# Memory values moved into the cross-attention, memory weights scaled in place on POOL, end of the mixer reordered, weight slots exchanged

## What is computed

```python
def mixer_layer(x, ...):
    h = rmsnorm(x, g) @ w_in_l           # split into q, k, v, hq, hf, hi, hg, cb, cc, ch
    a = attn(q, k, v)                    # block attention, prompt and sample rows
    o_h, S = hgrn2_mixer(hq, hf, hi, hg, ...)   # recurrence, per-head rmsnorm, silu(hg) as gate
    o_c = cb * causal_dwconv(cc * ch)
    return x + concatenate([a, o_h, o_c]) @ w_out_l

def memory_kv(mem, g, wk, wv):           # 256 memory rows of the prompt, per layer
    m = rmsnorm(mem, g)
    return m @ wk, m @ wv                # both are outputs too

def cross_attn(x, g, wq, wo, mk, mv):
    q = rmsnorm(x, g) @ wq
    p = softmax(q @ mk.T * scale)
    return (p @ mv) @ wo
```

## Time and profile before

| What | Value |
|---|---|
| Median of 3 runs | 884.84 us (880.19 to 889.64) |
| Profiled execution, its time and its span | 887.91 us, 886.1 us |
| Mean granted clock of the PE | 0.982 |
| PE busy | 838.4 us, 95% of the span |
| DVE busy | 580.1 us, 65% |
| ACT busy | 456.9 us, 52% |
| POOL busy | 363.3 us, 41% |
| Share of the PE in the chain that ended last | 67% |
| Moved by DMA | 137.70 MB, mean 155 GB/s |

### The profile page before, as it was taken

The page is one execution under the profiler, slowest core; times in us unless marked ns, Lnnn a source line. Parts: engine busy times, 40 slices in busy tenths (PEclk is TensorE's granted clock), DMA queues, the critical chain, the costliest instruction groups (busy, mean ns, idle before and its releaser), DMA issues.

```text
span 886.1 us, 17206 instructions
## 1 busy us (share of the span) xinstructions
PE 838.4 (95%) x6422; PEld 780.2 (88%) x6422; DVE 580.1 (65%) x1263; ACT 456.9 (52%) x944; POOL 363.3 (41%) x330
## 2 busy tenths in 40 slices
PE   8999999897898999999999998989889899999996
PEld 6988877785798999999999997779669899999996
DVE  4778864755798877735356887386469887763342
ACT  4653553537656656534345355353664775654332
POOL 1412310533225665666742241053212565566542
PEclk9999999999999999999999999999989999999998
DMA  9765621677165565555648663149825565655432
GB/s 276 198 161 162 191 73 48 174 198 227 49 191 143 163 172 156 166 168 166 185 122 204 185 190 97 49 126 236 230 55 144 145 183 149 177 157 163 159 107 73
DMA packets 210111, 137.70 MB, mean 155 GB/s; under 512 B 23764, under 2 KB 202620, under 8 KB 210028
## 3 DMA queue, kind: packets, MB, share of 16 engines
q1 hardware_dynamic: 201024, 113.56, 45.2%
q0 software_dynamic: 8544, 22.85, 8.8%
q10 hardware_dynamic: 459, 0.18, 0.1%
HBM read 131.13 MB, written 5.44 MB: 154 GB/s over the span
## 4 chain that ended last, share of the span: by engine, by line
PE 67%; DVE 11%; issue 9%; DMA 4%; ACT 3%; POOL 3%; DVEq 1%; POOLq 1%; SPq 0%; ACTq 0%
PE banks L1278 19%; PE banks L1280 18%; PE banks L1279 18%; DVE ring_r L1820 3%; DMA ring<-in_w_up 2%; PE banks L1273 2%; POOL XG L861 1%; PE banks L1517 1%; PE banks L1417 1%; DMA ring<-in_w_in 1%; DVE phase L2092 1%; DVE phase_r L1735 1%; PE banks L1622 1%; PE banks L1316 1%; POOL XG L849 1%
## 5 line engine op out<-in xcount | busy, mean ns | idle before, releaser
L1280 PE MATMUL banks<-mix_r,ring_r 128*128 128x288 f32 x960 | 283.9, 296 | 0.0
L1280 PEld LDWEIGHTS banks<-mix_r,ring_r 128*128 128x128 f32 x960 | 181.9, 190 | 0.0
L1278 PE MATMUL banks<-mix_r,ring_r 128*128 128x288 f32 x480 | 148.5, 309 | 9.9 <-issue 6.6
L914 POOL TENSOR_TENSOR ring_r<-ring,keysT_r 128x512 fp32r<-128x512 f32 (+2 forms) x36 | 100.2, 2784 | 110.2 <-ACT keysT_r L1158 103.0
L914 POOL TENSOR_TENSOR ring_r<-ring,vals_r 128x512 fp32r<-128x512 f32 (+2 forms) x32 | 88.8, 2775 | 93.9 <-ACT vals_r L1158 93.7
L1280 PE MATMUL banks<-phase_r,ring_r 128*128 128x288 f32 x416 | 122.6, 295 | 0.0
L1158 ACT CAST ring_r<-ring 128x1024 fp32r<-128x1024 f32 x60 | 62.4, 1047 | 90.6 <-DMA ring<-in_w_in 63.2
L1278 PEld LDWEIGHTS banks<-mix_r,ring_r 128*128 128x128 f32 x480 | 91.4, 190 | 16.6 <-issue 11.8
L1279 PE MATMUL banks<-XG_r,ring_r 128*128 128x288 f32 x352 | 104.5, 297 | 0.0
L2092 DVE SCALAR_TENSOR_TENSOR phase<-banks,fpar,phase 128x255 f32<-128x255 f32 (+1 forms) x160 | 76.7, 480 | 38.1 <-ACT phase L1214 31.7
L1820 DVE TENSOR_TENSOR ring_r<-ring,keysT_r 128x1536 fp32r<-128x1536 f32 (+1 forms) x36 | 59.6, 1656 | 54.1 <-ACT keysT_r L1158 54.1
(11 more groups left out here) (315 smaller groups left out, 2061.7 us busy)
## 6 DMA issues: line engine op xcount, KB each, us to landing
ring<-in_w_up SPq DMA_DIRECT2D x88, 512.0 KB, 5.3
ring<-in_w_in SPq DMA_DIRECT2D x36, 512.0 KB, 4.3
ring<-in_w_down SPq DMA_DIRECT2D x16, 1024.0 KB, 5.3
ring<-in_w_down SPq DMA_DIRECT2D x8, 768.0 KB, 4.8
rawk<-in_cache_k POOLq DMA_DIRECT2D x32, 128.0 KB, 3.0
vals<-in_cache_v POOLq DMA_DIRECT2D x32, 128.0 KB, 2.8
ring<-in_w_in SPq DMA_DIRECT2D x16, 256.0 KB, 4.1
rawk<-in_cache_mem_k POOLq DMA_DIRECT2D x16, 256.0 KB, 5.4
```

Of the source, the lines that this page charges most:

```text
L914: g_.tensor_tensor(lo[:, cols], both[:, cols], hi_part[:, cols].bitcast(F32), ALU.subtract).then_inc(w_lo_pool, 1)
L1278: mm(out_, hi_w, hi_x, start=start, stop=False)
L1280: return mm(out_, lo_w, hi_x, start=False, stop=stop)
```

## The change

Five edits, in one list:

1. The eight scalings of the memory by g (`mg`) are gone. POOL instead multiplies the four weight pieces of `mk` and `mv` in place by g (step `w_mem`), with one instruction of 128x1024 a piece, and the PE waits for that.
2. `mv` leaves the mixer. Its pieces are loaded last of all pieces, behind `xq`; its two products stand in the cross-attention, before `xt` 0 and behind `xt` 1, and `xov` waits until they are copied to SBUF. DVE instead of ACT empties `mv`, `turn_mk`, `cstate_out` and `ustate_in`; the last three stand behind `xov` now.
3. The end of the mixer is written in another order: `ss` among the `hg` products, `mk` 0 before `at` 3, the rounding and rest of the first two `out` pieces early, `ho` 0 before the convolution, `mk` 1 between the two halves of `ho`, `hn` 0 before the transposes `turn_ke`, the sample attention behind `hn`, and the gate multiplied in early on DVE. `MIXED_ORDER` puts the recurrence's two tiles last.
4. `vexp` is built right after the `hg` products instead of behind `mv`.
5. Slots 2 and 3 of the ring are exchanged for the pieces, and with them the products that SP waits for at the start of the second layer and for the first chunks.

```diff
-          + [("mk", (0,)), ("mk", (1,)), ("mv", (1,)), ("mv", (1,))]
-          + [("out", (m,)) for m in range(8)] + [("xq", (0,)), ("xq", (1,))])
+          + [("mk", (0,)), ("mk", (1,))] + [("out", (m,)) for m in range(8)]
+          + [("xq", (0,)), ("xq", (1,)), ("mv", (1,)), ("mv", (1,))])
...
-MIXED_ORDER = [6, 7, 4, 5, 0, 1, 2, 3]
+MIXED_ORDER = [6, 7, 0, 1, 2, 3, 4, 5]
...
+    for p in (P_MV, P_MV + 1):
+        a("op", "w_mem", p)
     for h in range(4):
         a("A", "xs", h)
     a("A", "ys")
...
     a("op", "ynorm")
-    a("A", "ustate_in", 0)
-    a("A", "ustate_in", 1)
+    a("D", "mv", 0)
     a("A", "xt", 0)
     a("A", "xt", 1)
     a("op", "round", "up", 0, l)
     a("op", "rest", "up", 0, l)
+    a("D", "mv", 1)
     a("A", "yt")
     a("A", "xov", 0)
     a("A", "xt", 2)
+    a("A", "xt", 3)
+    a("A", "yo")
+    a("A", "xov", 1)
+    for t in (0, 1):
+        a("D", "turn_mk", t)
+    a("D", "cstate_out")
+    a("A", "yot")
     a("op", "round", "up", 1, l)
     a("op", "rest", "up", 1, l)
-    a("A", "yo")
-    a("A", "xt", 3)
-    a("A", "yot")
-    a("A", "xov", 1)
+    a("D", "ustate_in", 0)
+    a("D", "ustate_in", 1)
     a("op", "round", "up", 2, l)
...
-        piece = [ring[:, 2 + q // 2, 1024 * (q % 2):1024 * (q % 2) + 1024] for q in range(4)]
+        piece = [ring[:, 3 - q // 2, 1024 * (q % 2):1024 * (q % 2) + 1024] for q in range(4)]
...
-                        sp.wait_ge(filled, (piece_use(l, P_XQ + 1), piece_use(l, P_OUT + 7), piece_use(l, P_OUT + 5),
-                                            piece_use(l, P_OUT + 7))[n])
+                        sp.wait_ge(filled, (piece_use(l, P_XQ + 1), piece_use(l, P_OUT + 5), piece_use(l, P_OUT + 7),
+                                            piece_use(l, P_MV + 1))[n])
...
+                elif step == "w_mem":
+                    p = args[0]
+                    if (l, p) == (0, P_MK):
+                        wait_emptied(pool, 0, "par")
+                    pool.wait_ge(piece_in[p % 4], piece_count[l, p])
+                    w = piece[p % 4].rearrange("p (k c) -> p k c", c=P)
+                    pool.drain()
+                    g_.tensor_tensor(w, w, par[:, par_col(R_MEM, l):par_col(R_MEM, l) + KT_D].unsqueeze(2).broadcast_to([P, KT_D, P]),
+                                     ALU.mult).then_inc(s["w_mem"], 1)
...
                 elif step == "mv":
                     t = args[0]
                     whole(l, P_MV)
                     whole(l, P_MV + 1)
-                    q = P_MV % 4
-                    w = ring[:, 2:4].rearrange("p s (h k c) -> p (s h) k c", h=2, c=P)[:, q:q + 2]
+                    assert P_MV % 4 == 2
+                    w = ring[:, 2].rearrange("p (h k c) -> p h k c", h=2, c=P)
                     for k in range(KT_D):
-                        last = mm(o[:, 0:256], mg[:, k, P * t:P * t + P], w[:, :, k], start=k == 0, stop=k == KT_D - 1)
+                        last = mm(o[:, 0:256], memT[:, k, P * t:P * t + P], w[:, :, k], start=k == 0, stop=k == KT_D - 1)
...
                 elif step == "xov":
                     p = args[0]
+                    wait_emptied(pe, l, "mv", 1)
```

131 lines of the change are left out of this document (64 added, 67 removed).

## The result

The changed kernel takes 906.67 us (median of 4 runs) beside 887.24 us for the kernel before (median of 4), a ratio of 1.0216 with a 95% interval of 1.017 to 1.0262: slower by 2.2%, and above the forecast range, which ended at 903. The profiled executions are 906.48 us with a span of 904.8 us now, and 887.91 us with 886.1 us before, so 18.7 us have to be found.

The account below looks back on a forecast made before the run. The PE, busy nearly all the span, was taken as the bound. First layer +3.95 and second +2.75 gave +6.7 us on 887.91, so 894.6, less 3.1 to the median: 891.5 us, 80% range 879 to 903.

Parts of the forecast that it names:

- The 7.0 us of `mv` leave the PE's queue: Mixer's end: without `mv` the first output product starts earlier, 8.0 us gained a layer, bounds 6.5 to 10.5.
- is not lost time: Mixer's end before the change: `mv`, 7.07 us on the PE, covers DVE's normalisation of the two halves of `ho`.
- Output projection, -3.6 and -1.7: Output projection: the PE's wait for memory keys goes, with its low clock in the first layer; 3.6 and 1.7 us gained.
- `vexp` moves to the end of the `hg` products, so POOL can load the keys: Output projection: keys load once the first output product frees the buffer, some 7 us before use, so the wait goes.
- Cross-attention, +15.55 and +12.45 with its low clock: Cross-attention: `mv` waits for POOL's scaled weights; 12.65 and 9.55 us lost, plus 2.9 a layer for low clock.
- The drain: Cross-attention, POOL before the first scaling: 3.5 us, taken between 2.44 after one store and 4.87 after four loads.
- The first: Rival, POOL in cross-attention: scalings of 5.5 us each, both layers lose 5.8 us more, 903 us; chance 0.30.
- The second: Rival, mixer: POOL's work stretches DVE's chain, gain falls to 5.5 us a layer, 896.5 us; chance 0.10.
- The third: Rival, cross-attention: scaled weights ready when scores end, `mv` covers the softmax wait, 870.5 us; chance 0.03.
- The fourth: Rival: mixer gain of 10.5 us and waits without low clock, 880.7 us, or 876 with fast POOL; chance 0.15.

Follow-up runs that it names:

- experiment 8: Changed kernel with the four `vexp` multiplications on POOL put behind the wait for `hstate`, ahead of its stores and the loads of memory keys; 902.46 us, ratio 1.0197.
- experiment 11: Changed kernel with 4 extra 128x256 products on the PE behind the wait for the second half of `ho`, before the first sample-attention output; 901.26 us, one run.
- experiment 12: As experiment 6, with POOL's scaling of the second `mk` piece held until the last group's first transposed probabilities are on the PE; 875.29 us, ratio 0.988.
- experiment 6: Changed kernel with the last two memory-value loads behind the scalings, 4 extra products before `hn`, second up chunk's rounding and `ustate_in` ahead of `yot`; 878.48 us, ratio 0.99.
- experiment 1: Changed kernel with POOL's last two loads of memory values moved behind the two scalings of the `mv` weights; 886.33 us, ratio 1.0004.

## Why the prediction was wrong

**The step that failed is "The 7.0 us of `mv` leave the PE's queue", priced at -8.0 a layer.** Measured: -2.5 and -0.9. Two ends of the chain behind it came out as written: DVE's second half of `ho` ended at 146.27 and the normalisation at 151.85, where 146.1 and 151.6 were written. That is in part luck, since POOL's work beside DVE is in it: without `vexp` there the normalisation ends 2.2 us earlier, counted from `level` 16 (experiment 8).

What failed is the length of the PE's work: every duration was taken at the high clock. `mv` was the run of full products in a stretch of small ones; without it the same work ran at the low level. From the second `hn` product to the first output product the changed kernel takes 10.1 us, and experiment 11, with 1.8 us more work, 7.6: the low clock costs 4.3 us there, and 4.2 in the second layer (582.28 to 592.31 against 7.6 again). The output products from there to the first `turn_cmem` take 4.5 us at the low clock, and 4.5 in experiments 11 and 12 at the high one, where they wait for the splits of the mixed tiles (0.35 us in the row at 154.38, then less at each); so the low clock costs nothing there in the first layer and 0.5 in the second. A short low stretch from 568.7 on costs the second layer another 1.6. The rest is POOL's work beside DVE, 1.4 us in each layer by experiments 6 and 12. With both mended the mixer's end is 8.2 and 8.3 us shorter than before (experiment 12): the 8.0 was there to be had, and the clock is most of what hid it. The prediction priced the low clock behind the waits of cross-attention and of the keys, and nowhere in the mixer; its sentence that `mv` "is not lost time" named one of the two things that `mv` covered. The miss of this term is 5.5 + 7.1 = 12.6 us, against 12.0 in the span.

The Trainium skill, page "TensorE: Matmul & The Clock Gate", section "HAM oscillation — how this bites in real kernels", tells of products that fall to the low clock because of the waits between them. For the wait of 10.83 us ahead of `mv` the trace agrees (0.51 over the stretch). For the mixer's end that account is not enough: the PE is 86% to 94% busy there, and in experiment 11 the wait of 1.6 us stayed and the clock did not fall.

**Output projection, -3.6 and -1.7: right in size, wrong in cause.** The wait for memory keys is gone (-3.8 and -2.0). The step says "`vexp` moves to the end of the `hg` products, so POOL can load the keys". By experiment 8 `vexp` may stand behind `hstate` and the keys are in time in the first layer and 0.49 us late in the second; what made it late before was in part the store of `mv` in front, which left with `mv`, and in part its own 6.22 us, 4.47 there.

**Cross-attention, +15.55 and +12.45 with its low clock: right in the sum (+16.4 and +12.1), by luck, with errors that cancel.** POOL's issuing ended at X + 12.9 as written. The drain took 7.38 and 5.97 us instead of 3.5, the scalings 1.89 each instead of 2.7, so `mv` 0 began at X + 24.4 and X + 22.9 instead of X + 22.0. The estimate of 2.25 us that the prediction made from the Trainium skill, page "GPSIMD Engine Reference", section 3.1, was nearer to 1.89 than the row that I chose. The drain was priced by how many DMAs stood ahead of it; its bound of 4.9 did not hold the value. The row was there to read otherwise: the store at 158.74 in front of `vexp` (in experiment 8 above) landed 3.0 us later, at 161.74, and `vexp` began at 161.97. From `mv` 0 to the up products 30.8 and 31.0 us passed, where 29.3 and 2.9 of low clock were forecast.

**The rivals.** The first (scalings of 5.5 us) gave the right side and nearly the right time by a mechanism that is not there: a scaling takes 1.89 (and its X + 27.8 adds up to X + 27.6). The second (POOL's work stretches DVE) is real and near its price of 2.5 us a layer: 1.4 us by experiment 12 beside 6, where the scaling is held, and 2.2 in the first layer by experiment 8, where `vexp` is gone; its place was the last head group's probabilities and not the chain that it named. The third (`mv` fills the waits) did not come about, but experiment 1 is on its way: the wait falls to 2.2 us. The fourth (chain nearly bare, no clock loss) fails on the clock. That the mixer's end itself could lose its clock was nobody's case, and the range ended at 903 because of that.

## What to carry to other kernels

Before a group of full matmuls is moved out of a stretch of small ones, look at what keeps the clock there: the busy share does not show it, the granted clock over the stretch does, and every duration of the new order has to be priced at either level. On POOL, arithmetic that is on the path and starts with a drain belongs ahead of the engine's own DMA issues, not behind them. Two ways to place work that look far apart (`mv` in the mixer or behind the scores) were worth the same once each had its two waits mended; the waits were the change, not the place.
